# Expert passes of a hybrid decoder step: an up ring of eleven slabs instead of eight, and TensorE's up loop as two turns of 22 slabs

## The chip, the cores and the metric

The kernel runs on one core of one Trainium2 chip. The metric is the device time of one execution in microseconds. The kernel is timed in several runs, of which the median counts.

## The reference, cut to what matters

Two decoder layers work on 288 tokens (256 of a prompt, 32 sampled) of width 1024. Each has a recurrent mixer; the first ends in a dense SwiGLU, the second in a mixture of eight SwiGLU experts of width 2816, of which each token takes its best two. The change lies in the second:

```
def swiglu(h, w1, w3, w2):
    return (jax.nn.silu(h @ w1) * (h @ w3)) @ w2

def moe_swiglu(h, router, w1, w3, w2):
    logits = (h @ router).astype(jnp.float32)
    top_v, top_i = lax.top_k(logits, TOP_K)
    probs = jax.nn.softmax(top_v, axis=-1)
    gate = jnp.sum(jax.nn.one_hot(top_i, N_EXPERTS, dtype=jnp.float32) * probs[..., None], axis=-2)
    out = jnp.zeros(h.shape, jnp.float32)
    for e in range(N_EXPERTS):
        out = out + gate[..., e:e + 1] * swiglu(h, w1[e], w3[e], w2[e]).astype(jnp.float32)
    return out.astype(h.dtype)
```

All numbers are float32.

## The kernel before, in words

The code is written engine by engine: each `@block` function is the program of one engine, in the order in which it stands, and semaphores tie them together. `mix_out` ends a layer's mixer (the branch and output projections, the router's logits); `experts` follows it in the second layer.

**Passes.** `experts` makes one pass per expert. A pass gathers the tokens of its expert into `hg` (8 blocks of 128 channels x `cap` columns), runs the up loop, the down loop, and adds the result to `xT`. The caps of the eight passes are 91, 88, 73, 85, 76, 82, 79 and 70 columns (`CAPS`), and a matmul takes longer with more columns. Seven passes (`FIXED`) are written out one behind the other in TensorE's program, with `pe.Fori` loops inside; the eighth stands in a loop whose count is read at run time (passes for overflowing experts; one is run here).

**Weights.** An expert's weights lie in DRAM as 68 slabs: `UP_SLABS` = 44 of 128 x 1024 numbers (w1 and w3 by turns: slab 2f and 2f+1 give hidden block f), and `DOWN_SLABS` = 24, of which every third is 128 x 768. Up slabs go to `ring` (`RING` = 8 slots; slab n to slot n % 8), down slabs to `down_ring` in `proj` (`DRING` = 6 slots). Each slot has a semaphore that counts arrivals (`slab_in`, `down_in`); `slab_done` counts the slabs that TensorE has used, over both kinds. All loads are issued by SyncE, in one order, each behind a wait for the `slab_done` that frees its slot: the pass's down slabs 0 to 5, its up slabs 8 to 43, then the up slabs 0 to 7 of the following expert (4 to 7 first: `FREED`), then this pass's down slabs 6 to 23. A load that has to wait holds up all that stand behind it.

**TensorE's up loop.** `up` waits for a slab and for a free bank, then `narrow_products` does 16 matmuls of 64 output rows. As float32 each is two weight loads and two matmul rows in the trace, so a slab is 32 matmul rows. The loop is `Fori(0, 5)` over 8 slabs, and a tail of four slabs. Product n goes to `bank[n % 4]`. ScalarE takes the even ones (`silu`, signals `w1_free`), VectorE multiplies the odd ones into `hid` (`w3_free`). VectorE also prepares the next gather matrix during the first nine blocks (`choose`).

**Behind the up loop** come three transposes (`scatter_matrix`), the gather of the next pass's tokens (`gather_tokens`, into `HG` = banks 4 to 7) and the down loop, `Fori(0, 4)`: two output blocks a turn of three slabs each (176 matmul rows a turn), then `add_up` and `to_tokens` for the blocks of the turn before.

`y_ret` holds an input of the mixer's gate products (`xsum_up`) until the third pair of slabs in `mix_out` is done; `lora_w` holds sums for the first pair. In `experts` neither is used.

Of the kernel before, what the change touches and what calls it, by code (L numbers as in the profile page):

```python
# [22 lines left out]
D = 1024  # L23
# [66 lines left out]
UP_SLABS = 2 * FT  # L90
DOWN_SLABS = 24
# [129 lines left out]
def build(nc, xT_in, w_mix, w_lora, w_rank, w_gkup, vec_in, vecf_in, router_in, w_ff, s_ret, s_gla, s_rw,  # L221
# [132 lines left out]
    slab_in = [nc.alloc_semaphore(name=f"slab_in{s}") for s in range(RING)]  # L354
    slab_done = nc.alloc_semaphore(name="slab_done")
# [81 lines left out]

    def load_ff_slab(sp, e, j, s, done, n=KT):
# [11 lines left out]
    def narrow_products(pe, s, out, rhs, n=KT, k0=0, last=KT):  # L450

        for k in range(n):
            for c in range(2):
                mm = nc.tensor.matmul(out[64 * c:64 * c + 64], ring[:, s, k, 64 * c:64 * c + 64], rhs[:, k0 + k, :],  # L454
                                      start=(k0 + k == 0), stop=(k0 + k == last - 1))
        mm.then_inc(slab_done, 1)
# [1667 lines left out]
    def mix_out(nc, block, sig, layer, delta, joined):  # L2124
# [32 lines left out]
        def _(sp):  # L2157
            load_group(sp, S_RW_OUT, 1)
            load_first_group(sp, S_OUT)
# [300 lines left out]
    def experts(nc, block, sig, layer, merge, rs):  # L2460
# [48 lines left out]
        def _(sp):  # L2509
            def freed_up(p, n):  # L2510

                if n >= RING:
                    return count(p, FF_SLABS, FF0 + n - RING + 1)
                return count(p, FF_SLABS, FF0 - FF_SLABS + max(range(n, UP_SLABS, RING)) + 1)

            def load_up(p, e, n):
                load_ff_slab(sp, e, n, n % RING, freed_up(p, n))
# [10 lines left out]
            for q in range(FIXED):  # L2528
# [3 lines left out]
                for n in range(RING, UP_SLABS):  # L2532
# [4 lines left out]
                for n in FREED:  # L2537
# [5 lines left out]
            with sp.Fori(0, rest) as i:  # L2543
# [5 lines left out]
                for n in range(RING, UP_SLABS):  # L2549
                    load_up(p, e, n)  # L2550
                for n in FREED:
                    sp.wait_ge(slab_done, freed_up((i, FIXED + 1), n))
                    settle(sp)
                    sp.dma_start(ring[:, n], w_ff[following, n]).then_inc(slab_in[n], 16)
# [6 lines left out]
            for s in range(RING):  # L2561
                per = len(range(s, UP_SLABS, RING))
                fill = fills_before(layer, s) + fills(len(STREAM), s) + FIXED * per + 1
                sp.wait_ge(slab_in[s], rest * (per * 16) + fill * 16)
# [3 lines left out]
        def _(pe):  # L2568
# [741 lines left out]
```

## Time and profile before

| what | value |
|---|---|
| median of 3 runs | 2516.02 us (2513.42 to 2517.08) |
| profiled execution | 2513.11 us |
| its span in the profile | 2511.3 us |
| TensorE matmul busy | 2442.6 us, 97% |
| VectorE, ScalarE busy | 51%, 24% |
| granted TensorE clock | 0.997 of full |
| DMA moved in the span | 500.85 MB, mean 199 GB/s |

The profile is of one execution. The span runs from its first to its last instruction; the rest of the execution's time lies around it. TensorE's busy share counts a matmul as busy from its start to a modelled end, so gaps between matmuls are what shows of its waits. In the last quarter of the span the page shows DMA engines that are busy for eight to nine tenths or more, and 340 to 400 GB/s; before that they are busy for two to six tenths.

### The profile page before, as it was taken

To read this page: it belongs to the slowest core of one execution; us is meant where nothing else is said; L and a number is where in the kernel's file an instruction comes from. 1 tells how busy PE (TensorE), PEld (TensorE's weight loads), DVE (VectorE), ACT (ScalarE), POOL (GpSimd) and SP (SyncE) were. 2 spreads that over 40 slices of the span, in tenths; PEclk is the share of its full clock that TensorE was granted. 3 is DMA by queue.
4 is the path that set the end of the run, shared out by engine and by line. 5 is a ranking of instruction groups with operands and counts; after the bars stand their busy time and mean duration, and the time that the engine had idled before them with its cause. 6 is when DMAs were issued, how large, how long until landed. Compare 5 with 4: busy or idle time off the path is not lost. (4 is left out here: it accounts for less than half of the span.)

```text
span 2511.3 us, 103490 instructions
## 1 busy us (share of the span) xinstructions
PE 2442.6 (97%) x45930; PEld 2040.3 (81%) x45930; DVE 1291.6 (51%) x3328; ACT 609.9 (24%) x1798; POOL 0.2 (0%) x4
## 2 busy tenths in 40 slices
PE   9999999999999999999999999999999999999997
PEld 7987666666699999998766666678999899888986
DVE  7666666666686676756576666667311111111111
ACT  2233333433311101233333334421111111111111
POOL 0000000000000000000000000000000000000000
PEclk9999999999999999999999999999999999999999
DMA  6334442222243454333353222234899999999997
GB/s 248 111 136 161 151 133 88 83 83 79 99 154 136 153 173 144 128 124 139 129 168 129 84 78 77 83 112 154 341 342 390 393 392 370 402 372 374 402 388 274
DMA packets 146091, 500.85 MB, mean 199 GB/s; under 512 B 18784, under 2 KB 23520, under 8 KB 143360
## 3 DMA queue, kind: packets, MB, share of 16 engines
q1 hardware_dynamic: 145792, 496.44, 54.7%
q8 instruction: 239, 3.92, 0.6%
q14 instruction: 60, 0.49, 0.1%
HBM read 476.08 MB, written 20.29 MB: 198 GB/s over the span
## 5 line engine op out<-in xcount | busy, mean ns | idle before, releaser
L301 PE MATMUL psum<-hT,ring 128*64 128x144 f32 (+1 forms) x4568 | 457.4, 346 | 3.7 <-DVE hT L2421 1.7
L454 PE MATMUL psum<-work,ring 128*64 128x91 f32 (+7 forms) x11264 | 422.0, 234 | 15.7 <-issue 7.3
L454 PEld LDWEIGHTS psum<-work,ring 128*64 128x64 f32 x11264 | 404.7, 136 | 33.3 <-issue 23.8
L301 PEld LDWEIGHTS psum<-hT,ring 128*64 128x64 f32 x4568 | 293.3, 137 | 96.2 <-issue 12.1
L2958 DVE TENSOR_TENSOR work<-psum,work 128x91 f32<-128x91 f32 x176 | 44.6, 253 | 365.4 <-PE psum L454 365.2
L2661 PE MATMUL psum<-work,proj 128*64 128x91 f32 (+7 forms) x5632 | 208.9, 234 | 10.6 <-issue 9.2
L2661 PEld LDWEIGHTS psum<-work,proj 128*64 128x64 f32 x5632 | 202.3, 137 | 16.1 <-issue 10.3
L1767 ACT ACTIVATE work<-psum 128x256 f32<-128x256 f32 (+4 forms) x320 | 104.1, 362 | 349.7 <-PE psum L1678 84.8
L301 PE MATMUL psum<-work 128*64 128x144 f32 (+4 forms) x2096 | 154.1, 282 | 4.3 <-DVE work L1258 3.6
L301 PE MATMUL psum<-y_ret,work 128*64 128x144 f32 x2400 | 156.3, 286 | 0.5 <-DVE y_ret L531 0.5
L301 PEld LDWEIGHTS psum<-y_ret,work 128*64 128x64 f32 x2400 | 148.7, 137 | 0.9 <-issue 0.9
L2949 DVE TENSOR_TENSOR xT<-xT,psum 128x288 f32<-128x288 f32 x64 | 29.1, 455 | 228.6 <-PE psum L2672 227.6
L301 PEld LDWEIGHTS psum<-work 128*64 128x64 f32 (+2 forms) x2096 | 121.3, 136 | 30.6 <-issue 11.3
L2744 ACT ACTIVATE work<-psum 128x91 f32<-128x91 f32 x176 | 43.5, 247 | 377.5 <-PE psum L454 377.5
L301 PE MATMUL psum<-y_ret,ring 128*64 128x144 f32 (+1 forms) x1280 | 126.8, 332 | 2.5 <-ACT work L1767 2.5
L301 PEld LDWEIGHTS psum<-y_ret,ring 128*64 128x64 f32 x1280 | 79.5, 137 | 18.4 <-ACT work L1767 4.5
L323 PE MATMUL psum<-hT,ring 128*128 128x288 f32 x252 | 72.8, 408 | 0.0
L2748 ACT ACTIVATE work<-psum 128x91 f32<-128x91 f32 x64 | 15.9, 248 | 228.1 <-PE psum L2661 228.1
L1563 PEld LDWEIGHTS psum<-work 64*64 64x64 f32 x1408 | 47.3, 134 | 29.4 <-issue 17.7
L546 DVE TENSOR_TENSOR y_gla<-psum,y_gla 128x288 f32<-128x288 f32 x72 | 33.0, 458 | 72.8 <-PE psum L301 72.2
L301 PE MATMUL psum<-hT,work 128*64 128x144 f32 x928 | 68.8, 287 | 0.0
L518 DVE TENSOR_TENSOR work<-ring 128x512 f32<-128x512 f32 (+1 forms) x90 | 54.7, 608 | 19.0 <-PE psum L301 19.0
(513 smaller groups left out, 3733.5 us busy)
## 6 DMA issues: line engine op xcount, KB each, us to landing
ring<-w_ff_dram SPq DMA_DIRECT2D x424, 512.0 KB, 7.3
ring<-w_mix_dram SPq DMA_DIRECT2D x256, 512.0 KB, 4.1
proj<-w_ff_dram SPq DMA_DIRECT2D x128, 512.0 KB, 5.3
proj<-w_ff_dram SPq DMA_DIRECT2D x64, 384.0 KB, 5.6
work<-s_gla_dram SPq DMA_DIRECT2D x8, 1024.0 KB, 5.3
gla_s_out<-work SPq DMA_DIRECT2D x8, 1024.0 KB, 4.7
work<-s_ret_dram SPq DMA_DIRECT2D x8, 512.0 KB, 5.4
ret_s_out<-work SPq DMA_DIRECT2D x8, 512.0 KB, 3.0
```

Source lines behind the costliest of these rows:

```text
L301: last = nc.tensor.matmul(out[64 * c:64 * c + 64], weights[:, 64 * c:64 * c + 64], x, start=start, stop=stop)
L323: mm = (in_halves if self.narrow else nc.tensor.matmul)(out, ring[:, s, k, :], rhs[:, k, :], start=(k == 0), stop=(k == KT - 1))
L454: mm = nc.tensor.matmul(out[64 * c:64 * c + 64], ring[:, s, k, 64 * c:64 * c + 64], rhs[:, k0 + k, :], start=(k0 + k == 0), stop=(k0 + k = ...
L518: op.tensor_tensor(s1, a21, a22, ALU.add).then_inc(sig("wsum"), 1)
L546: nc.vector.tensor_tensor(c[:, 1:3, :], two(LAST_TWO[side]), c[:, 5:7, :], ALU.add).then_inc(sig("outer"), 1)
L1563: last = mm(unit(half(W, r), c), half(AT, 1 - r)[:, c], half(X, 1 - r)[:, c], start=True, stop=True)
L1767: return nc.scalar.activation(out, in_, func, **kw)
L2661: last = mm(DOWN[m][64 * h:64 * h + 64, 0:cap], down_ring[:, d, k, 64 * h:64 * h + 64], hid[:, KT * c + k, 0:cap], start=(KT * c + k == 0) ...
L2744: ac(act1[:, f % 2, :], bank[2 * f % 4][:, 0:CAP], ACT.Silu).then_inc(sig("w1_free"), 1)
L2748: ac(oT[:, m % 2, :], DOWN[m % 2][:, 0:CAP], cp).then_inc(sig("oT"), 1)
L2949: tt(xT[:, k, :], xT[:, k, :], ADD[m % 2][:, 0:T], ALU.add).then_inc(sig("added"), 1)
L2958: tt(hid[:, f, :], bank[(2 * f + 1) % 4][:, 0:CAP], act1[:, f % 2, :], ALU.mult).then_inc(sig("w3_free"), 1)
```

## The change

The up ring gets three more slots: `y_ret` (two) and `lora_w` (one). `UP_RING` = 11, slab n goes to slot n % 11, and 44 is four rounds of it. The three slots are filled for expert 1 in `mix_out`, behind a wait for the third gate pair (`join_done(BRANCH0 - 1)`). SyncE's order stays, with 11 for 8: down 0 to 5, up 11 to 43, the following expert's up 0 to 10, down 6 to 23. TensorE's up loop becomes `Fori(0, 2)` over 22 slabs (`TURN`) without a tail. The pairs of products still alternate between banks 0-1 and 2-3, but each eleventh pair goes to banks 6-7, which adds waits for "otok" and "added" of the pass before ahead of slab 20 of a turn. The gather is done in two halves (banks 4 and 5, then 6 and 7), with the wait for the last product's evacuation before the second half, where it had stood behind the gather. `narrow_products` uses `in_halves`, with the same matmuls in the same order (so their line is L303 in the changed kernel, not L454).

```diff
+UP_RING = 11
+TURN = 2 * UP_RING
...
+    extra_in = [nc.alloc_semaphore(name=f"extra_in{s}") for s in range(UP_RING - RING)]
+    up_in = slab_in + extra_in
...
+    extra_slots = [x.rearrange("p k n -> p (k n)")[:, D * j:D * j + D].rearrange("p (k n) -> p k n", k=KT)
+                   for x, j in ((y_ret[:, :, :], 0), (y_ret[:, :, :], 1), (lora_w[:, :, :], 0))]
+    up_slots = [ring[:, s] for s in range(RING)] + extra_slots
...
             load_group(sp, S_RW_OUT, 1)
+            if not dense:
+                sp.wait_ge(slab_done, join_done(BRANCH0 - 1))
+                for n in range(RING, UP_RING):
+                    sp.dma_start(up_slots[n], w_ff[1, n]).then_inc(up_in[n], 16)
             load_first_group(sp, S_OUT)
...
+        UP_BANK = [bank[6:8] if f % UP_RING == UP_RING - 1 else bank[0:2] if f % UP_RING % 2 == 0 else bank[2:4]
+                   for f in range(FT)]
...
-        FREED = 4, 5, 6, 7, 0, 1, 2, 3
...
-                if n >= RING:
-                    return count(p, FF_SLABS, FF0 + n - RING + 1)
-                return count(p, FF_SLABS, FF0 - FF_SLABS + max(range(n, UP_SLABS, RING)) + 1)
+                if n >= UP_RING:
+                    return count(p, FF_SLABS, FF0 + n - UP_RING + 1)
+                return count(p, FF_SLABS, FF0 - FF_SLABS + UP_SLABS - UP_RING + n + 1)
...
-                for n in range(RING, UP_SLABS):
+                for n in range(UP_RING, UP_SLABS):
                     load_up(p, e, n)
...
-                for n in FREED:
+                for n in range(UP_RING):
                     load_up((0, q + 1), following, n)
...
-            def gather_tokens(n, cap):
+            def gather_tokens(n, cap, evacuated=None):
 
                 pe.wait_ge(sig("picked"), n)
-                for j in range(2):
-                    for r in range(4):
-                        rows = slice(NS * r, NS * r + NS)
-                        mm(HG[r][:, CAP * j:CAP * j + cap], htok2[rows, j, :], gather[rows, 2, 0:cap], start=(j == 0),
-                           stop=False)
                 for r in range(4):
+                    if r == 2 and evacuated is not None:
+                        pe.wait_ge(sig("w3_free"), evacuated)
+                    if r % 2 == 0:
+                        for j in range(2):
+                            for q in range(r, r + 2):
+                                rows = slice(NS * q, NS * q + NS)
+                                mm(HG[q][:, CAP * j:CAP * j + cap], htok2[rows, j, :], gather[rows, 2, 0:cap],
+                                   start=(j == 0), stop=False)
...
-                narrow_products(pe, s, bank[n % 4][:, 0:cap], hg[:, :, 0:cap])
+                if n == TURN - 2:
+                    pe.wait_ge(sig("otok"), count(p, KT, 2))
+                    pe.wait_ge(sig("added"), count(p, KT, 2))
+                narrow_products(UP_BANK[f][n % 2][:, 0:cap], up_slots[s], hg[:, :, 0:cap])
...
-                with pe.Fori(0, UP_SLABS // RING) as g:
-                    for n in range(RING):
+                with pe.Fori(0, UP_SLABS // TURN) as g:
+                    for n in range(TURN):
                         up(p, cap, n, g)
-                for n in range(UP_SLABS // RING * RING, UP_SLABS):
-                    up(p, cap, n, 0)
                 scatter_matrix(p)
-                pe.wait_ge(sig("otok"), count(p, KT, 2))
-                pe.wait_ge(sig("added"), count(p, KT, 2))
-                gather_tokens(count(p, 1, 2), next_cap)
-                pe.wait_ge(sig("w3_free"), count(p, FT, FT + 2))
+                gather_tokens(count(p, 1, 2), next_cap, count(p, FT, FT + 2))
```

TensorE's program of pass 1, before: the loop body is 128 matmuls between the two branches, then the tail of 64, the transposes (L2648) and the gather.

```order
L2685 UNCONDITIONAL_BRANCH
...
L454 MATMUL psum<-work,ring 64x91 x32
L2638 REGISTER_ALU
L454 MATMUL psum<-work,ring 64x91 x32
...
L454 MATMUL psum<-work,ring 64x91 x32
...
L454 MATMUL psum<-work,ring 64x91 x32
L2685 REGISTER_ALU
L2685 COMPARE_AND_BRANCH
L454 MATMUL psum<-work,ring 64x91 x64
L2648 MATMUL psum<-table,work 91x128 x2
...
L2619 MATMUL psum<-work 128x88 x8
L2626 MATMUL psum<-work 64x88 x32
```

The same place in the changed program. Between the branches stand 352 matmuls now, with the slots in `y_ret` and `lora_w` among them, and nothing is left behind the loop but transposes and the gather in two halves.

```order
L2706 UNCONDITIONAL_BRANCH
...
L303 MATMUL psum<-work,ring 64x91 x32
...
L303 MATMUL psum<-work,y_ret 64x91 x32
L2656 REGISTER_ALU
L303 MATMUL psum<-work,lora_w 64x91 x16
...
L303 MATMUL psum<-work,lora_w 64x91 x16
L2706 REGISTER_ALU
L2706 COMPARE_AND_BRANCH
L2669 MATMUL psum<-table,work 91x128 x2
...
L2638 MATMUL psum<-work 128x88 x4
L2644 MATMUL psum<-work 64x88 x16
L2638 MATMUL psum<-work 128x88 x4
L2644 MATMUL psum<-work 64x88 x16
```

SyncE's queue between two passes, before: the last of the following expert's eight up slabs, and then this pass's down slabs from number 6 on.

```order
L441 DMA ring<-w_ff_dram 128x1024
L441 ISA
L441 DMA ring<-w_ff_dram 128x1024
L441 ISA
L441 DMA ring<-w_ff_dram 128x1024
L2525 ISA
L2525 DMA proj<-w_ff_dram 128x1024
L2525 ISA
L2525 DMA proj<-w_ff_dram 128x1024
...
L2525 DMA proj<-w_ff_dram 128x768
```

The same place now. The up slabs end with the three new slots, number 8 to 10 of the following expert, and they stand ahead of down slab 6.

```order
L2533 DMA ring<-w_ff_dram 128x1024
L2533 ISA
L2533 DMA ring<-w_ff_dram 128x1024
L2533 ISA
L2533 DMA y_ret<-w_ff_dram 128x1024
L2533 ISA
L2533 DMA y_ret<-w_ff_dram 128x1024
L2533 ISA
L2533 DMA lora_w<-w_ff_dram 128x1024
L2541 ISA
L2541 DMA proj<-w_ff_dram 128x1024
...
L2541 DMA proj<-w_ff_dram 128x768
```

What moved: down slab 6 stands behind eleven up slabs instead of eight.

## Rows read from the trace of the kernel before

**Rows 1.** The page, section 1: engine, busy us, share of the span, instructions
```profile
PE 2442.6 (97%) x45930; PEld 2040.3 (81%) x45930; DVE 1291.6 (51%) x3328; ACT 609.9 (24%) x1798; POOL 0.2 (0%) x4
```

**Rows 2.** The page's DMA issues: count, KB each, median us from issue to landing
```profile
ring<-w_ff_dram SPq DMA_DIRECT2D x424, 512.0 KB, 7.3
...
proj<-w_ff_dram SPq DMA_DIRECT2D x128, 512.0 KB, 5.3
proj<-w_ff_dram SPq DMA_DIRECT2D x64, 384.0 KB, 5.6
```

**Rows 3.** Groups by line, 1765 to 2511 us: busy, mean ns | idle before
```profile
L454 PE MATMUL psum<-work,ring 128*64 128x91 f32 (+7 forms) x11264 | 422.0, 234 | 15.7 <-issue 7.3 <-DMA ring<-w_ff_dram 5.2
```

**Rows 4.** Stretches: window, length, busy by engine, clock, DMA share, GB/s
```profile
1826.70:1865.10 38.40, 37.76 (x831) 34.44 (x829) 5.11 (x13) 4.07 (x17) 0.00 (x0) 1.00 0.92 319
...
1956.60:2009.80 53.20, 50.91 (x1410) 47.14 (x1409) 8.65 (x29) 8.03 (x26) 0.00 (x0) 1.00 1.02 406
2009.80:2043.80 34.00, 32.48 (x829) 28.87 (x827) 5.08 (x13) 4.03 (x16) 0.00 (x0) 1.00 1.00 383
```

**Rows 5.** Timeline of TensorE: start, us, line, count [idle before <- releaser]
```profile
1770.80 55.95 PE L454 MATMUL psum<-work,ring 128*64 128x91 f32 x1408 [0.20 <-issue]
...
1956.63 7.20 PE L454 MATMUL psum<-work,ring 128*64 128x73 f32 x219
1964.19 12.36 PE L454 MATMUL psum<-work,ring 128*64 128x73 f32 x357 [0.37 <-issue]
...
1987.03 10.00 PE L454 MATMUL psum<-work,ring 128*64 128x73 f32 x256 [0.24 <-DMA ring<-w_ff_dram]
1997.27 12.56 PE L454 MATMUL psum<-work,ring 128*64 128x73 f32 x320 [0.24 <-DMA ring<-w_ff_dram]
2009.76 0.65 PE L2648 MATMUL psum<-table,work 128*91 128x128 f32 x3
...
2022.22 5.80 PE L2661 MATMUL psum<-work,proj 128*64 128x73 f32 x176
...
2043.81 7.26 PE L454 MATMUL psum<-work,ring 128*64 128x85 f32 x190
...
2135.43 5.50 PE L454 MATMUL psum<-work,ring 128*64 128x76 f32 x160
...
2223.86 4.91 PE L454 MATMUL psum<-work,ring 128*64 128x82 f32 x130
2230.20 4.72 PE L454 MATMUL psum<-work,ring 128*64 128x82 f32 x126 [1.43 <-issue]
2236.62 41.50 PE L454 MATMUL psum<-work,ring 128*64 128x82 f32 x1120 [1.70 <-issue]
2279.61 1.36 PE L454 MATMUL psum<-work,ring 128*64 128x82 f32 x32 [1.48 <-DMA ring<-w_ff_dram]
...
2316.93 20.39 PE L454 MATMUL psum<-work,ring 128*64 128x79 f32 x576
...
2406.05 6.21 PE L454 MATMUL psum<-work,ring 128*64 128x70 f32 x194 [0.91 <-issue]
```

**Rows 6.** DMA queues (packets, MB, share): 1865-2405, 140-230, 2275.9-2277.0, 2277.0-2278.1 (two), 2278.1-2279.2
```profile
q8 instruction: 32, 0.52, 0.4%
...
q1 hardware_dynamic: 3501, 11.39, 35.0%
...
q1 hardware_dynamic: 126, 0.45, 102.8%
...
q1 hardware_dynamic: 118, 0.43, 98.4%
q8 instruction: 1, 0.02, 6.1%
...
q1 hardware_dynamic: 119, 0.44, 101.3%
```

**Rows 7.** Timeline of SyncE's queue, 1640 to 1760 us
```profile
1702.01 21.38 SPq L422 DMA_DIRECT2D ring<-w_mix_dram  x8
```

More of the change, by code:

```diff
@@ L448, in slab_products, with narrow_products @@
         mm.then_inc(slab_done, 1)
[L450 to L455, printed above, removed]
+    def narrow_products(out, slab, rhs):
+        for k in range(KT):
+            mm = in_halves(out, slab[:, k, :], rhs[:, k, :], k == 0, k == KT - 1)
         mm.then_inc(slab_done, 1)
@@ L2548, in _ @@
                     load_down(p, e, d)
-                for n in range(RING, UP_SLABS):
+                for n in range(UP_RING, UP_SLABS):
                     load_up(p, e, n)
-                for n in FREED:
+                for n in range(UP_RING):
                     sp.wait_ge(slab_done, freed_up((i, FIXED + 1), n))
                     settle(sp)
-                    sp.dma_start(ring[:, n], w_ff[following, n]).then_inc(slab_in[n], 16)
+                    sp.dma_start(up_slots[n], w_ff[following, n]).then_inc(up_in[n], 16)
                 for d in range(DRING, DOWN_SLABS):
@@ L2560, in _ @@
             sp.wait_ge(sig("stored"), 4 * 16)
[L2561 to L2564, printed above, removed]
+            for s in range(UP_RING):
+                per = UP_SLABS // UP_RING
+                sp.wait_ge(up_in[s], rest * (per * 16) + (up_fills(s) + FIXED * per + 1) * 16)
                 settle(sp)
@@ L2633, in up @@
                 i, done = p
-                s = n % RING
-                per = len(range(s, UP_SLABS, RING))
-                fill = fills_before(layer, s) + fills(len(STREAM), s) + done * per + n // RING + 1
-                pe.wait_ge(slab_in[s], turn * 16 + (i * (per * 16) + fill * 16))
-                pe.wait_ge(sig("w3_free" if n % 2 else "w1_free"), turn * (RING // 2) + count(p, FT, n // 2 + 1))
+                s, f = n % UP_RING, n // 2
+                per = UP_SLABS // UP_RING
+                fill = up_fills(s) + done * per + n // UP_RING + 1
+                pe.wait_ge(up_in[s], turn * (TURN // UP_RING * 16) + (i * (per * 16) + fill * 16))
+                pe.wait_ge(sig("w3_free" if n % 2 else "w1_free"), turn * UP_RING + count(p, FT, f + 1))
                 if n in (2, 3):
                     pe.wait_ge(sig("oT"), count(p, KT, n - 1))
-                narrow_products(pe, s, bank[n % 4][:, 0:cap], hg[:, :, 0:cap])
+                if n == TURN - 2:
+                    pe.wait_ge(sig("otok"), count(p, KT, 2))
+                    pe.wait_ge(sig("added"), count(p, KT, 2))
+                narrow_products(UP_BANK[f][n % 2][:, 0:cap], up_slots[s], hg[:, :, 0:cap])
             def scatter_matrix(p):
                 pe.wait_ge(sig("gated"), count(p, 1, 1))
-                pe.wait_ge(sig("w3_free"), count(p, FT, FT + 1))
+                pe.wait_ge(sig("w3_free"), count(p, FT, FT))
                 for i, (a, n) in enumerate(TILES):
```

9 lines of the change are left out of this document (6 added, 3 removed).

## The prediction

> **What bounds the kernel now.** I read the page first: TensorE is busy for 97% of the span [rows 1], so nothing but its own waits can be won. The change touches only the eight expert passes, which begin at 1770.80 us [rows 5] and fill nearly all that is left of the span, so nearly every view after that is of this stretch. The DMA issues on the page give the slab sizes: 512 KB, and 384 KB for every third down slab [rows 2]. The groups by line say that the up matmuls (L454) lost 15.7 us in idle time, of which 7.3 us is "issue" (nothing that the profile shows was waited for) and 5.2 us a wait for a ring slab [rows 3]. That is all that stands in front of these matmuls as gaps; smaller waits are smeared between them.
>
> The stretches tell which resource is full. In the up loop of pass 3 (73 columns) the DMA share is 1.02 at 406 GB/s, and in its down part 1.00 at 383 GB/s: the queue never rests there. In the down part of pass 1 it is 0.92, so it rests a little there [rows 4]. The timeline gives the price of a slab: in the starved middle of pass 3 eight slabs (256 matmul rows) start 10.24 us apart (1987.03 and 1997.27), so 1.28 us each [rows 5]. A pass loads 44 up and 24 down slabs. If the small ones cost as much as the large, that is 68 x 1.28 = 87.0 us. Pass 3 lasts from 1956.63 to 2043.81, 87.2 us [rows 5], so the **ledger of the queue closes** at this price, and 383 GB/s at a full share in the down part agrees (fewer bytes in the same time). Pass 5 lasts 88.4 us, pass 6 93.1 us, pass 7 89.1 us [rows 5].
>
> The second thing in the timeline is the "issue" gap. In pass 6 TensorE stops for 1.43 us after 130 matmul rows and for 1.70 us after 126 more [rows 5]. Each matmul row has a weight load beside it, so 128 rows are 256 instructions, and the instruction queue q8 moves 32 packets with 0.52 MB in six passes, 16 KB each [rows 6], which is 256 instructions of 64 bytes. So these gaps are waits for the next block of TensorE's program. In passes 2 to 7 that is 5.3 blocks a pass, while TensorE executes far more instructions than that: loop bodies are not fetched again. How long a block takes to come: pass 6 entered one at about 2223.9 and went on at 2230.20 (6.3 us), entered the next at 2230.20 and went on at 2236.62 (6.4 us); pass 3 entered one after 91 of its 219 rows, at 1959.6, and went on at 1964.19 (4.6 us); pass 1 runs through all 1408 rows without a gap, and 128 of its rows take 5.1 us, so there it was at most 5.1 us [rows 5]. I take 5.3 us, with 4.6 and 6.4 as ends.
>
> **The ring, part by part.** Eleven slots instead of eight let three more up slabs (3.84 us of queue time) wait ready. They do not make the queue faster, and its order matters: the next pass's eleven up slabs are issued before down slab 6 of this pass. In a pass that the queue bounds, every pass still has to load 68 slabs between the same two points, so it stays at 87.0 us. Worked through for pass 3: its last up slab begins when it lands, 1997.27 plus 288 of 320 rows, 2008.6. Down slab 6 lands 8 + 1 slabs later, 2020.1, and TensorE takes it at 2022.22 [rows 5]. With eleven slots the last up slab lands three slabs earlier, 2004.7, but down slab 6 twelve slabs after that, again at 2020.1; TensorE, 3.8 us earlier, now wants it at 2018.4 and **waits 1.7 us in the down loop**. The rest is given back behind it. So what the ring can return is the time by which a pass exceeds 87.0 us because of the queue: pass 3 0.2, pass 5 1.4, pass 7 2.1; pass 6 the 1.48 us that it waited for its last up slab, and 0.9 us smeared over 1120 rows (36.9 ns each against 36.1 ns in the 126 rows before) [rows 5]. Passes 4 and 8, whose gaps are not taken apart here, I take like pass 5. Together 8.9 us; the lower end is 0. I take half, 4.4 us, since the down wait above eats into each.
>
> **The three extra loads ahead of pass 1** stand behind a wait that is one slab earlier than what the S_OUT loads wait for. Those eight loads are released one by one over 21.4 us [rows 7], 2.7 us or more each against 1.28 us of queue time, and each is used eight slabs after the release: 3.84 us are hidden there, 0. Pass 8 loads three slabs more that nobody uses, behind the up slabs and ahead of down slab 6: 3.84 us of queue, which cancels against the three loaded early.
>
> **The turn of 22 slabs.** The old body is 8 slabs, 256 matmul rows, two block borders, and the five turns reuse it. The new body is 704 rows, 5.5 blocks, walked once with fetching and once, if it stays, without: **3.5 more borders and 2.5 more blocks a pass** (a block in the tail of four slabs goes away). At a border TensorE waits 5.3 us less the time that 128 rows take. Where TensorE is the bound: pass 1 (5.1 us) 0.2, passes 2 and 4 (88 and 85 columns, between pass 1 and pass 6's 4.8 us, so 4.9) 0.4 each, together 1.0 x 3.5 = 3.5 us. In the passes that the queue bounds the wait itself is covered: at 73 columns four slabs take 4.2 us and the queue needs 5.1 us for them; if that cover went, it would be 1.1 x 3.5 = 3.9 us a pass. But there the block's packet takes queue time. In the 1.1 us around the one at 2277 us the slab queue's share falls from 102.8 to 98.4, while the block's own packet takes 6.1%, 1.07 us of one engine [rows 6]. Against the mean of the stretches before and after (102.8 and 101.3) it is 3.65%, which over 1.1 us is 0.64 us of one engine. If every slab waits for that engine a block costs 0.64 us; pass 3, with five blocks and a ledger that closes to 0.2 us, says 0.04 us. I take 0.3 us, between the two: 2.5 x 5 passes x 0.3 = 3.8 us (0.5 to 8.0).
>
> TensorE's program has four turns of looping less a pass; nothing shows at the old loop ends (1408 rows in one piece in pass 1 [rows 5]), so 0. The gather in two halves has the same matmuls; its new wait is for the vector product of the last slab, which runs beside the transposes (0.65 us [rows 5]) and the first half of the gather: 0. The third bank pair (6 and 7) for each eleventh product waits for "otok" and "added" of the pass before, done some 20 slabs earlier: 0.
>
> **Sum.** -4.4 + 3.5 + 3.8 = +2.9 us. The profiled execution took 2513.11 us (span 2511.3 us), so 2516.0 us by its own time; it lies 2.9 us under the median of the runs, 2516.02 us, and by the median it is **2519 us**.
>
> **Does the body stay?** In the stretch from 140 to 230 us TensorE repeats a loop of 261 matmuls with their loads (4.3 blocks by the same count), and no instruction packet moves at all: the only queue there is q1 [rows 6]. So at least 4.3 blocks stay; 5.6 are needed. By the Trainium skill (Runtime: NRT & Kernel Launch, Instruction fetch mechanics) TensorE's instruction memory holds 128 KiB, 2048 instructions, in 16 KiB blocks, while the same section says that the memory is only two such lines and that a taken branch out of the window stalls for a fetch. By the first the new body stays and the sum is as above; by the second each turn would be fetched again. The 4.3 blocks speak against the second.
>
> **Rivals.** *The body is fetched again in the second turn.* Then 44 slabs are eleven blocks at 5.3 us and the jump back waits for a whole one: 58.3 + 5.3 = 63.6 us for an up loop that takes 53 to 57 us now, about 8 us more in each of eight passes: 2580 us. For it: nothing as long as 5.6 blocks has been looped. Chance 0.06.
>
> *Faster.* The ring returns all 8.9 us and the borders are hidden (a block takes 5.0 us or less, as in pass 1): 2507 us. For it: in pass 6 both gaps come early, while the ring is full and the queue rests, and the wait for the last slab comes late; three more slots join them. Against it: the down wait worked out above. Chance 0.25.
>
> *Slower, by the blocks.* With up to eleven slabs on the way instead of eight, and in the middle of the up loop rather than at its start, a block comes later. At 5.8 us the borders of passes 1, 2, 4 and 6 cost (0.7 + 0.9 + 0.9 + 1.0) x 3.5 = 12.3 us, the packets 5 us, less 4.4 us: +12.9, 2529 us. It decides from about 5.5 us on. Pass 6 showed 6.3 and 6.4 us. With 6.4 us and 0.64 us a packet it is +24 us. Chance 0.31.
>
> **Chances.** The forecast (within a few microseconds of no change) has 0.38. 0.2% is 5 us, about what a measurement of this kernel can tell from no change. Faster 0.25, same 0.38, slower 0.31 + 0.06 = 0.37. The range reaches from the full return of the ring, 2507, to a little past the slower case, 2532; outside lie the refetching case, 0.06, and the tails of the two others, about 0.1. The likeliest case's own range is 2511 to 2521.
>
> **What would show it.** The gaps before L454 (now at L303) from a ring slab should nearly vanish from the up loops of passes 3, 5 and 7, and new waits for a proj slab appear before the third block of the down loop. q8 should move about 7.9 packets a pass instead of 5.3, all the added ones in the first 22 slabs, none in the second 22. In pass 1 small "issue" gaps should appear every 128 rows of the first turn, and pass 3 should still last 87 us. The prediction is wrong if queue-bound passes fall well below 87 us (then the ledger is no floor), if packets show up in the second turn, or if the gaps at borders are well above 1 us in passes 1 and 2.

## The result, and the profile after

The changed kernel takes 2528.55 us (median of 9 runs, 2521.68 to 2534.41), the kernel before 2514.55 us (9 runs, 2511.73 to 2517.08). The ratio is 1.0054, with an interval of 1.0042 to 1.0066: the change **costs 13.6 us**. The forecast was 2519 us with a range of 2507 to 2532: the time lies in the range, but 9.5 us above the forecast, where the rival "slower, by the blocks" (2529) stood. A few executions of some kernels in this document ran at a lower clock or far longer than the rest; they are left out of every time and ratio. The profiled execution has a span of 2526.7 us and a granted clock of 0.993.

The page after the change, TensorE, the instruction queue and the down matmuls:

```profile
PE 2438.6 (97%) x45930; PEld 2046.1 (81%) x45930; DVE 1290.6 (51%) x3328; ACT 609.1 (24%) x1798; POOL 0.2 (0%) x4
...
q8 instruction: 260, 4.26, 0.7%
...
L2682 PE MATMUL psum<-work,proj 128*64 128x91 f32 (+7 forms) x5632 | 212.8, 237 | 12.8 <-issue 6.8
```

TensorE is busy for 4 us less than in [rows 1] in a span that is 15.4 us longer, so its idle time grew by 19.4 us. The view of waits for 1765 to 2530 us (engine, line, releaser: us in total, times, longest) names it:

```profile
PE psum L303 <- issue: 34.1, 29, 3.0
...
PE psum L2682 <- issue: 6.8, 6, 2.0
...
PE psum L2682 <- DMA proj<-w_ff_dram: 5.4, 6, 2.4
```

In [rows 3] the up matmuls waited 7.3 us for "issue" and 5.2 us for a ring slab. Now it is 34.1 us for "issue", and no wait for a slab is left in any up loop. The ring does what it was made for, but the waits for "issue", which the prediction put down to blocks of TensorE's program, grew by far more than the ring removed. And the waits for down slabs are 5.4 us, where the same view of the kernel before has 1.0 us.

TensorE's timeline in passes 1 and 3 (start, us, line, count [idle before <- releaser]):

```profile
1782.79 1.88 PE L303 MATMUL psum<-work,y_ret 128*64 128x91 f32 x42 [0.22 <-issue]
...
1788.64 8.38 PE L303 MATMUL psum<-work,ring 128*64 128x91 f32 x205 [0.64 <-issue]
...
1800.21 0.93 PE L303 MATMUL psum<-work,y_ret 128*64 128x91 f32 x18 [1.43 <-issue]
...
1962.71 6.69 PE L303 MATMUL psum<-work,ring 128*64 128x73 f32 x204
1969.67 1.87 PE L303 MATMUL psum<-work,ring 128*64 128x73 f32 x52 [0.27 <-issue]
...
1976.39 0.92 PE L303 MATMUL psum<-work,lora_w 128*64 128x73 f32 x22 [2.50 <-issue]
...
1982.77 4.21 PE L303 MATMUL psum<-work,ring 128*64 128x73 f32 x125 [0.53 <-issue]
1988.28 1.11 PE L303 MATMUL psum<-work,ring 128*64 128x73 f32 x28 [1.30 <-issue]
...
2003.44 8.30 PE L303 MATMUL psum<-work,ring 128*64 128x73 f32 x256
...
2028.67 7.30 PE L2682 MATMUL psum<-work,proj 128*64 128x73 f32 x176 [0.54 <-DMA proj<-w_ff_dram]
```

Each of the "issue" gaps stands some 128 rows (or twice that) behind the one before it, and all in the first turn. From one gap to the next is taken here as the time that a block took to come: in pass 1 5.85 us (1782.79 to 1788.64) and then 11.57 us for two; in pass 3 6.7, 6.4 and 5.5 us. Other passes spread further: in pass 5 the gaps end at 2149.77, 2154.89 and 2162.24 us, so 5.1 and 7.4 us. The second turn of pass 3 runs without a gap (256 rows from 2003.44 in 8.30 us, 32.4 ns each). The DMA queues of pass 3, its first turn (1962.7 to 1992.3) and its second (1992.3 to 2014.7), say the same:

```profile
q1 hardware_dynamic: 3022, 10.88, 96.0%
q8 instruction: 5, 0.08, 1.1%
...
q1 hardware_dynamic: 2457, 8.95, 101.5%
```

Five blocks in the first turn, none in the second. The first turn also shows the slab queue at 96.0% only. Stretches of the changed kernel (window, length, busy by engine, clock, DMA share, GB/s): the up loop of pass 1, up loop and down part of pass 3, two stretches inside its first turn, and one down turn each of passes 3, 5 and 8:

```profile
1771.40:1830.30 58.90, 56.61 (x1408) 56.06 (x1408) 12.38 (x55) 6.22 (x23) 0.00 (x0) 1.00 0.95 360
1962.70:2014.70 52.00, 47.40 (x1409) 46.78 (x1408) 8.62 (x29) 7.69 (x26) 0.00 (x0) 0.97 0.99 383
2014.70:2052.20 37.50, 34.67 (x831) 30.91 (x827) 5.08 (x13) 4.34 (x16) 0.00 (x0) 0.95 1.00 385
1960.00:1975.00 15.00, 13.62 (x377) 12.59 (x374) 3.83 (x10) 3.20 (x9) 0.00 (x0) 1.00 0.96 363
1975.00:1990.00 15.00, 11.79 (x305) 11.48 (x306) 2.47 (x8) 1.23 (x5) 0.00 (x0) 0.89 0.98 370
...
2028.70:2036.00 7.30, 7.30 (x178) 7.25 (x180) 0.00 (x0) 0.25 (x1) 0.00 (x0) 0.79 0.97 378
...
2212.20:2219.90 7.70, 7.69 (x178) 7.64 (x180) 0.00 (x0) 0.25 (x1) 0.00 (x0) 0.78 0.99 374
...
2487.30:2495.50 8.20, 8.16 (x178) 8.09 (x180) 0.00 (x0) 0.25 (x1) 0.00 (x0) 0.68 0.92 328
```

The two 15 us windows of the kernel before, for comparison, and then when a block comes: the first 5 us of pass 1 before, and a stretch between two gaps of pass 1 after:

```profile
1960.00:1975.00 15.00, 14.52 (x442) 14.10 (x438) 4.54 (x13) 1.73 (x7) 0.00 (x0) 1.00 1.02 398
1975.00:1990.00 15.00, 14.07 (x380) 12.74 (x376) 1.87 (x7) 1.49 (x6) 0.00 (x0) 1.00 1.03 410
...
1770.80:1776.00 5.20, 5.20 (x131) 5.20 (x133) 4.23 (x29) 0.49 (x2) 0.00 (x0) 1.00 0.49 147
...
1783.00:1788.60 5.60, 5.01 (x126) 4.82 (x122) 0.97 (x4) 0.49 (x2) 0.00 (x0) 1.00 1.03 414
```

Where the queue moved 398 and 410 GB/s it now moves 363 and 370. At the start of an up loop the ring is full and the queue has little to do (a share of 0.49 in pass 1 before); the blocks of the long turn come later, at a share of 1.03.

**The gather** has the same matmuls as before, but in two halves they take longer. Behind the up loop of pass 1, before and after:

```profile
1827.07 0.74 PE L2619 MATMUL psum<-work 32*128 32x88 f32 x16
1827.75 2.65 PE L2626 MATMUL psum<-work 128*64 128x88 f32 x64
...
1830.72 0.74 PE L2638 MATMUL psum<-work 32*128 32x88 f32 x8
1831.40 1.44 PE L2644 MATMUL psum<-work 128*64 128x88 f32 x32
1832.76 0.68 PE L2638 MATMUL psum<-work 32*128 32x88 f32 x8
1833.37 1.43 PE L2644 MATMUL psum<-work 128*64 128x88 f32 x32
```

Eight of the 32-partition rows take as long as sixteen did (0.68 us to the next line). Before, four groups of 32 partitions came by turns, now two. From the first transpose to the first down matmul it is 4.31 us in place of 3.54 in pass 1, and 0.75 to 0.77 us more in each of passes 1 to 3 and 5 to 7: up to 6 us in the eight passes, wherever TensorE is what bounds.

**The clock.** The three windows of the kernel after at 0.79, 0.78 and 0.68 show that after a wait TensorE comes back at a lower granted clock: 176 rows take 7.30 us that took 5.80 us in [rows 5]. An estimate of the whole from the mean clocks: 0.7% of a span of 2526.7 us is 17.7 us of full clock that was not granted, 0.3% of 2511.3 us is 7.5 us, so at most some 10 us of the 15.4 us lie in the clock (the rounding of the clocks leaves 2 to 3 us either way). It is hardly a cause of its own beside the waits: in these windows it falls behind them.

The passes by the timeline, from start to start, in us (pass 8: to the end of its last down matmul; ring of ten: the second experiment):

| pass | 1 | 2 | 3 | 4 | 5 | 6 | 7 | 8 | sum |
|---|---|---|---|---|---|---|---|---|---|
| before | 94.3 | 91.6 | 87.2 | 91.6 | 88.4 | 93.1 | 89.1 | 89.3 | 724.6 |
| after | 97.2 | 94.1 | 89.5 | 91.5 | 92.6 | 91.2 | 92.5 | 90.4 | 739.0 |
| ring of ten | 94.3 | 92.1 | 86.4 | 90.7 | 88.8 | 89.4 | 88.8 | 86.6 | 717.1 |

Six of the eight passes lose, those bound by TensorE (1, 2) and those bound by the queue (3, 5, 7) among them. Of the 2.9 us in pass 1 the up loop lost 3.1 us (59.0 in place of 55.9) and the gather 0.8, and the down loop, which has no gap now, gave back 0.9.

### The profile page after: what moved, and what is told of

Its sections match the earlier page's. It is cut to its first block and busy times, and to the rows that moved or that the text cites. A ratio compares the mean times of both kernels' runs of the same rounds, so it can differ in the third digit from the quotient of the medians.

```text
span 2526.7 us, 103445 instructions
## 1 busy us (share of the span) xinstructions
PE 2438.6 (97%) x45930; PEld 2046.1 (81%) x45930; DVE 1290.6 (51%) x3328; ACT 609.1 (24%) x1798; POOL 0.2 (0%) x4
## 5 line engine op out<-in xcount | busy, mean ns | idle before, releaser
L303 PE MATMUL psum<-hT,ring 128*64 128x144 f32 (+1 forms) x4568 | 457.5, 346 | 3.7 <-DVE hT L2435 1.7
L303 PE MATMUL psum<-work,ring 128*64 128x88 f32 (+8 forms) x8800 | 350.7, 238 | 21.6 <-issue 21.5
L303 PEld LDWEIGHTS psum<-hT,ring 128*64 128x64 f32 x4568 | 293.4, 137 | 96.1 <-issue 12.0
L303 PEld LDWEIGHTS psum<-work,ring 128*64 128x64 f32 x8800 | 335.4, 138 | 25.8 <-issue 24.7
L303 PE MATMUL psum<-work 128*64 128x144 f32 (+4 forms) x2096 | 154.2, 282 | 4.3 <-DVE work L1268 3.6
L303 PE MATMUL psum<-y_ret,work 128*64 128x144 f32 x2400 | 156.3, 286 | 0.5 <-DVE y_ret L541 0.5
L303 PEld LDWEIGHTS psum<-y_ret,work 128*64 128x64 f32 x2400 | 148.8, 137 | 0.9 <-issue 0.9
L303 PEld LDWEIGHTS psum<-work 128*64 128x64 f32 (+2 forms) x2096 | 121.4, 136 | 30.6 <-issue 11.3
L303 PE MATMUL psum<-y_ret,ring 128*64 128x144 f32 (+1 forms) x1280 | 126.9, 332 | 2.5 <-ACT work L1777 2.5
L303 PEld LDWEIGHTS psum<-y_ret,ring 128*64 128x64 f32 x1280 | 79.6, 137 | 18.4 <-ACT work L1777 4.5
L303 PE MATMUL psum<-work,y_ret 128*64 128x91 f32 (+7 forms) x2048 | 80.1, 233 | 5.1 <-issue 5.1
L303 PEld LDWEIGHTS psum<-work,y_ret 128*64 128x64 f32 x2048 | 76.0, 136 | 6.3 <-issue 6.1
L1573 PEld LDWEIGHTS psum<-work 64*64 64x64 f32 x1408 | 47.3, 134 | 29.4 <-issue 17.7
```

The source lines that it names most:

```text
L303: last = nc.tensor.matmul(out[64 * c:64 * c + 64], weights[:, 64 * c:64 * c + 64], x, start=start, stop=stop)
L1573: last = mm(unit(half(W, r), c), half(AT, 1 - r)[:, c], half(X, 1 - r)[:, c], start=True, stop=True)
```

## The experiments

**Two theories.** *The blocks* (the prediction's slower rival): what costs is the longer stretch of program that each pass walks through for the first time; the ring itself gains. *The order*: what costs is that eleven up slabs instead of eight stand ahead of down slab 6, which showed as the 5.4 us of waits for `proj`. A pass's program for the up loop counts here as slabs written out: 12 before (8 + 4), 22 after; each adds 64 instructions, so ten slabs are 2.5 blocks a pass and 20 in eight passes.

**1. Blocks without the ring.** In the kernel before, the first turn of eight slabs is written out ahead of the loop: 20 slabs, two blocks a pass more.

```diff
-                with pe.Fori(0, UP_SLABS // RING) as g:
-                    for n in range(RING):
+                for n in range(RING):
+                    up(p, cap, n, 0)
+                with pe.Fori(0, UP_SLABS // RING - 1) as g:
+                    for n in range(RING, 2 * RING):
```

> The kernel before (ring of eight, same loads) with the first turn of eight slabs written out ahead of a loop of four turns: two more blocks of TensorE's program a pass, nothing else. Theory A (the program blocks cost the time: waits at block borders, and their packets in the queue): two of the 2.6 added blocks, so 8 to 12 us above the kernel before, TensorE's issue waits in front of the up matmuls about 20 us instead of 7.3 us. Theory B (the ring's three slabs ahead of down slab 6 cost it, the program is harmless): no change, 0 to 2 us.

Measured: 2520.77 against 2512.96 us, ratio 1.0030 (1.0020 to 1.0041). The waits of its expert passes:

```profile
PE psum L454 <- issue: 22.9, 18, 2.4
...
PE psum L454 <- DMA ring<-w_ff_dram: 2.1, 11, 0.2
```

So blocks alone cost 7.5 us (5.0 to 10.3), 0.47 us each. The "issue" waits grew by 15.6 us, but the profiled execution, 2526.81 us, is one of the longest of its kernel, 13.7 us above the profiled one of the kernel before; and with eight slots TensorE had been waiting for slabs anyway: 3.1 of those 5.2 us are gone here.

**2. The ring without the blocks.** Ten slots need no long turn: 44 slabs are four turns of ten and a tail of four, 14 slabs written out, half a block a pass more than before. The early loads, the gather in halves and the third bank pair are in it too. Since 44 is not a multiple of ten, the following expert's slabs are again loaded in the order in which their slots come free (`FREED`).

```diff
-UP_RING = 11
+UP_RING = 10
...
-        UP_BANK = [bank[6:8] if f % UP_RING == UP_RING - 1 else bank[0:2] if f % UP_RING % 2 == 0 else bank[2:4]
+        UP_BANK = [bank[6:8] if f % 5 == 4 else bank[0:2] if f % 5 % 2 == 0 else bank[2:4]
...
-                with pe.Fori(0, UP_SLABS // TURN) as g:
-                    for n in range(TURN):
+                with pe.Fori(0, UP_SLABS // UP_RING) as g:
+                    for n in range(UP_RING):
                         up(p, cap, n, g)
+                for n in range(UP_SLABS // UP_RING * UP_RING, UP_SLABS):
+                    up(p, cap, n, 0)
```

> A ring of ten (two slots more than before), with the up loop as four turns of ten slabs and a tail of four: half a block more than before instead of 2.6. Theory A: within 4 us of the kernel before, issue waits about 10 us. Theory B: two of the three slabs stand ahead of down slab 6, so 8 to 10 us above before, with the waits for a proj slab at 3 to 5 us.

Measured: 2506.62 us, ratio 0.9976 (0.9968 to 0.9985), **6.0 us faster than before** and the best kernel of this study. Its waits, and then its stretches of pass 3 (up loop, down part):

```profile
PE psum L302 <- issue: 10.1, 11, 2.3
...
PE psum L2682 <- DMA proj<-w_ff_dram: 2.9, 6, 1.1
PE psum L302 <- DMA ring<-w_ff_dram: 1.5, 7, 0.3
```

```profile
1959.88:2010.96 51.08, 49.41 (x1409) 46.58 (x1408) 8.62 (x29) 7.98 (x26) 0.00 (x0) 1.00 1.02 402
2010.96:2046.32 35.36, 33.39 (x832) 29.52 (x828) 5.10 (x13) 4.08 (x17) 0.00 (x0) 1.00 1.02 395
```

The up loop is 2.1 us shorter than in [rows 4] and the down part 1.4 us longer; pass 3 as a whole goes from 87.2 to 86.4 us. That is the ledger of the queue at work, as it was worked out for eleven slots (0.8 us of the 1.4 us is the gather in halves). The gain comes from passes that were longer than the ledger: pass 6 93.1 to 89.4, pass 8 89.3 to 86.6. Not all of it need be the ring's: in pass 6 the "issue" gaps of the up loop fell from 3.1 to 0.6 us, since block borders fell elsewhere; over all passes such waits hardly changed (17.9 to 18.7 us).

**3. The order.** In the changed kernel, up slabs 8 to 10 of the following expert go behind down slab 11.

```diff
-                for n in range(UP_RING):
+                for n in range(RING):
                     load_up((0, q + 1), following, n)
-                for d in range(DRING, DOWN_SLABS):
+                for d in range(DRING, 2 * DRING):
+                    load_down(p, e, d)
+                for n in range(RING, UP_RING):
+                    load_up((0, q + 1), following, n)
+                for d in range(2 * DRING, DOWN_SLABS):
```

> The changed kernel with SyncE's order changed: the following expert's up slabs 0 to 7, then down slabs 6 to 11, then up slabs 8 to 10, then down 12 to 23. Theory A: the waits for a proj slab fall from 5.4 us to about 1 us, but the issue waits of the up loop stay near 27 us, and the time stays within 5 us of the changed kernel (10 us or more above before). Theory B: most of the 13.6 us comes back, 2 to 5 us above before.

Measured: 2539.64 us, ratio 1.0112 (1.0097 to 1.0127), worse by another 14.6 us. Its waits:

```profile
PE psum L303 <- issue: 34.8, 31, 2.7
PE psum L2692 <- DMA proj<-w_ff_dram: 19.0, 10, 2.7
```

The waits for down slabs grow from 5.4 to 19.0 us, where the first theory had expected about 1 us and the second most of the loss back. Down slabs 6 to 11 wait for slots that TensorE frees only as it works through the down loop, and SyncE's queue holds up the three up slabs, whose slots are free, behind them. Slabs that can go at once belong ahead of slabs that must wait. The order theory falls with this order and with experiment 2, which has ten slabs ahead of down slab 6 and gains.

**4. Fewer instructions for the same work.** In the changed kernel the up matmuls are 128 wide, which halves their instructions.

```diff
-            mm = in_halves(out, slab[:, k, :], rhs[:, k, :], k == 0, k == KT - 1)
+            mm = nc.tensor.matmul(out, slab[:, k, :], rhs[:, k, :], start=(k == 0), stop=(k == KT - 1))
```

> The changed kernel with up matmuls of 128 output rows instead of two of 64: half as many instructions a slab, so the first turn has 2.75 blocks instead of 5.5. A matmul row then takes about twice as long (16 rows of the final sums took 4.16 us for 288 columns, so 82 ns at 91 columns, 1.32 us a slab against 1.27 us). Theory A: the border waits nearly vanish, since a block lasts 10 us; passes bound by the queue fall towards 87 us and the others gain the borders and lose 2 us: 2508 to 2518 us. Theory B: slower than the changed kernel by the longer matmuls, 2530 to 2535 us.

Measured: ratio 1.0744 (1.0726 to 1.0763), about 2700 us (2697.55 to 2703.04 in three runs). The profiled execution took 2772.80 us: its granted clock is 1.00 up to 2400 us and falls to 0.54 in the last 140 us of the passes. The "issue" waits in front of the up matmuls fall to 1.2 us, as they should by the blocks. But the work itself became dearer, as the group by line and the start of pass 1 show:

```profile
L465 PE MATMUL psum<-work,ring 128*128 128x91 f32 (+7 forms) x4096 | 513.3, 293 | 1.2 <-issue 1.2
...
1771.36 14.52 PE L465 MATMUL psum<-work,ring 128*128 128x91 f32 x128 [0.23 <-issue]
```

At the full clock 128 rows of 91 columns take 14.36 us (to the next line, 1785.72), 112 ns a row, in place of two narrow rows at 39.7 ns (1408 in 55.9 us); the 125 ns a row of the group hold the stretch at the lower clock. By the ratio, the wide rows cost 171 us more than the narrow ones of the changed kernel, and 33 us more still for the waits they saved: 204 us over 5632 rows, 36 ns a row more than two narrow ones. My price for a wide row, 82 ns, was wrong, and this way to fewer blocks is closed.

**5 and 6. Half the up bytes.** Both kernels load only the first four of the eight channel blocks of each up slab in the passes and leave out the rest; TensorE does the same matmuls. The edit in the changed kernel (the kernel before passes 4 to its `load_ff_slab`):

```diff
-                sp.dma_start(up_slots[n % UP_RING], w_ff[e, n]).then_inc(up_in[n % UP_RING], 16)
+                sp.dma_start(up_slots[n % UP_RING][:, 0:4], w_ff[e, n, :, 0:4]).then_inc(up_in[n % UP_RING], 16)
```

> The kernel before, but each up slab of the passes (other than the first eight) loads only its first 4 of 8 blocks, so that the queue is never full in the up loop; TensorE multiplies what the slot still holds in the other half. Theory A (a program block comes late because the weight loads fill the DMA engines): no waits for slabs and no issue waits in front of the up matmuls at two borders a pass; about 40 us below the kernel before, 2470 to 2480 us. If a block takes its time whatever the queue does: the 7 us of issue waits stay.

> The changed kernel with the same halved up loads. Theory A: the borders cost nothing when the queue is not full, so it takes the same time as the kernel before with halved loads (within 3 us) and its issue waits in the up loop fall from 27 us more than before to about none. If a block takes 5 us whatever the queue does: about 20 us of issue waits stay and it is 10 to 20 us slower than the kernel before with halved loads.

Measured: before 2466.73 us (0.9820, 0.9803 to 0.9837), after 2479.61 us (0.9865, 0.9851 to 0.9879). By the ratios the difference between them is 11.3 us, where the theory had expected less than 3. But not all of it is blocks: with TensorE the bound (no pass of the two waits for an up slab) the gather in halves costs its 0.75 us in each (28.4 in place of 23.1 us over the first seven passes), 6.0 us in eight. That leaves some 5 us, about 0.25 us for each of the 20 blocks, with no ring waits for the ring to return. Pass 3 of the second, up loop and down part:

```profile
1958.40:2005.80 47.40, 45.74 (x1409) 45.14 (x1408) 8.61 (x29) 7.69 (x26) 0.00 (x0) 1.00 0.79 259
2005.80:2040.40 34.60, 33.27 (x831) 29.30 (x827) 5.07 (x13) 4.35 (x16) 0.00 (x0) 1.00 0.85 311
```

At a share of 0.79 the up matmuls of all passes wait 8.5 us for "issue" instead of 34.1 (3.0 us in the kernel before with half the bytes). The up loop of pass 1 takes 55.9 us, as in the kernel before, instead of 59.0: there a block costs nothing without the full queue. In pass 3 it still costs (44.9 us without, 47.4 us with the long turn): 128 rows of 73 columns take 4.1 us, and its blocks took 5.4 and then 4.3 us. So a block's cost has two parts, and the full queue adds the larger: 0.25 us a block without it, 1.1 us with it and the deeper ring (experiment 7).

**7. The blocks on top of the good ring.** The kernel of experiment 2, with its first turn of ten written out: 24 slabs, 20 blocks more.

```diff
-                with pe.Fori(0, UP_SLABS // UP_RING) as g:
-                    for n in range(UP_RING):
+                for n in range(UP_RING):
+                    up(p, cap, n, 0)
+                with pe.Fori(0, UP_SLABS // UP_RING - 1) as g:
+                    for n in range(UP_RING, 2 * UP_RING):
...
-                if n == UP_RING - 2:
+                if n % UP_RING == UP_RING - 2 and n < 2 * UP_RING:
```

> The ring of ten with its first turn of ten slabs written out ahead of a loop of three: 2.5 more program blocks a pass than the ring of ten, about as many as the changed kernel has. Theory A: those blocks cost 8 to 11 us, so the 6 us that the ring of ten gained become a loss of 2 to 5 us against the kernel before. Theory C (the ring of eleven is worse for its eleventh slab or for its third bank pair, not for its blocks): no change against the ring of ten, 5 to 7 us below before.

Measured: 2528.41 us, ratio 1.0065 (1.0049 to 1.0081). Its waits:

```profile
PE psum L302 <- issue: 30.0, 27, 2.3
...
PE psum L2682 <- DMA proj<-w_ff_dram: 2.2, 3, 1.0
```

It loses 22 us to the ring of ten (more than either theory expected), 1.1 us a block, and lands where the changed kernel did, with fewer waits for down slabs than that. The eleven slots, the slot in `lora_w` and the turn of 22 as such are not needed to explain the loss.

**8. A ring of twelve.** Three turns of twelve and a tail of eight: 20 slabs, 12 blocks more than the ring of ten, and two slots more (the second new one in `lora_w`). An even number of pairs a turn needs no third bank pair.

```diff
-UP_RING = 10
+UP_RING = 12
...
-        UP_BANK = [bank[6:8] if f % 5 == 4 else bank[0:2] if f % 5 % 2 == 0 else bank[2:4]
+        UP_BANK = [bank[0:2] if f % 2 == 0 else bank[2:4]
```

> A ring of twelve (four slots more, a second one in the same dead buffer as the eleventh), three turns of twelve slabs and a tail of eight: two more program blocks a pass than before, like the kernel with the peeled turn, and more ring than the changed kernel. Theory A: the blocks cost about 7 us and the ring gives back 4 to 6 us, so 0 to 5 us above before. Theory B (slabs ahead of down slab 6 cost it): worse than the changed kernel, 15 us or more above before.

Measured: 2518.50 us, ratio 1.0026 (1.0017 to 1.0035): 12.6 us above the ring of ten, 1.05 us a block. Waits of L302 for "issue" are 21.5 us.

**9. All 44 slabs written out** in the kernel before: eight blocks a pass more, 64 in all.

```diff
-                with pe.Fori(0, UP_SLABS // RING) as g:
-                    for n in range(RING):
-                        up(p, cap, n, g)
-                for n in range(UP_SLABS // RING * RING, UP_SLABS):
+                for n in range(UP_SLABS):
```

> The kernel before (ring of eight) with all 44 up slabs written out and no loop: eight more program blocks a pass, 64 in all. If a block costs the same wherever it is crossed, at 0.5 us (as the peeled turn says) 30 us above before, at 1.1 us (as the peeled ring of ten says) 70 us. If only the first turn's borders matter (ring full, queue at rest) and later borders are covered by the wait for slabs, it saturates at 10 to 20 us above before.

Measured: 2574.42 us, ratio 1.0240 (1.0225 to 1.0255), 60 us, 0.94 us a block. Waits and the instruction queue of the expert passes:

```profile
PE psum L454 <- issue: 74.5, 63, 2.8
...
q8 instruction: 108, 1.77, 0.8%
```

108 packets against 60 in experiment 1 over the same passes: 48 more, as six blocks a pass should give. The blocks' price does not shrink with their number; it is twice that of experiment 1.

**10. A gentler order for the ring of ten.** Its last two up slabs go behind down slabs 6 and 7.

```diff
-                for n in FREED:
+                for n in FREED[:RING]:
                     load_up((0, q + 1), following, n)
-                for d in range(DRING, DOWN_SLABS):
+                for d in range(DRING, DRING + 2):
+                    load_down(p, e, d)
+                for n in FREED[RING:]:
+                    load_up((0, q + 1), following, n)
+                for d in range(DRING + 2, DOWN_SLABS):
```

> The ring of ten with SyncE's order changed a little: the following expert's eight first-freed up slabs, then down slabs 6 and 7, then the two last up slabs, then down 8 on. Down slab 6 no longer stands behind more up slabs than in the kernel before, and the two up slabs wait only until two down slabs are used. If the waits for proj slabs (2.9 us) are what the ring gives back: 1 to 3 us below the ring of ten. If holding up slabs behind down slab 7 lets the queue rest, as in the coarser change of order: 0 to 5 us above it.

Measured: 2517.22 us, ratio 1.0014 (1.0005 to 1.0024), 9.5 us slower than without, where 1 to 3 us less or up to 5 us more had been expected. Its waits (in a profiled execution of 2512.63 us, one of its shortest):

```profile
PE psum L2692 <- DMA proj<-w_ff_dram: 11.3, 14, 2.1
PE psum L302 <- issue: 9.2, 12, 1.4
```

The waits for down slabs rise from 2.9 to 11.3 us here too.

Together, by slabs written out in a pass (intervals above; every ring of ten or more has the gather in halves, those of eight have not, so each price compares like with like):

| kernel | slots | slabs written out | ratio to before | a block costs |
|---|---|---|---|---|
| ring of ten | 10 | 14 | 0.9976 | |
| before | 8 | 12 | 1 | |
| ring of twelve | 12 | 20 | 1.0026 | 1.05 us (to ring of ten) |
| first turn written out | 8 | 20 | 1.0030 | 0.47 us (to before) |
| the change | 11 | 22 | 1.0054 | 1.2 us (to ring of ten) |
| ring of ten, first turn written out | 10 | 24 | 1.0065 | 1.1 us (to ring of ten) |
| all written out | 8 | 44 | 1.0240 | 0.94 us (to before) |

## Why the prediction was right in its range and wrong in its sum

**What the number is worth.** 2528.55 us lies in the range of 2507 to 2532 because the range reached out to the slower rival; the sum itself, 2519, and the likeliest case's own range, 2511 to 2521, missed it. That the rival's 2529 fits is in part luck: it put 3.2 and 3.5 us on the borders of passes 4 and 6, which came out 0.1 and 1.8 us shorter than before, and only packets (5 us in five passes) on the queue-bound ones, of which passes 3, 5 and 7 lost 2.3, 4.1 and 3.4 us.

**What held.** The mechanism of most parts: the waits for ring slabs vanished; q8 moved five packets in pass 3's first turn and none in its second, 47 in six passes, 7.8 each against 7.9 foretold; the body of 5.6 blocks stays. The new wait for a down slab stands where it was put, before the third block of pass 3's down loop (0.54 us after the change, behind an "issue" gap of 1.75 us in the turn before; 1.10 us in the ring of ten; 1.7 us worked out). The early loads and the third bank pair show no wait of their own; no run has them alone. The queue's ledger is a floor: no pass of any kernel with whole slabs is more than 1 us below 87.0 us (86.4 the lowest).

**The step that failed** is the one on the borders: "in the passes that the queue bounds the wait itself is covered". It priced the 20 added blocks at 3.5 + 3.8 = 7.3 us. They cost some 22 to 24 us. This comes from two sides: the ring of ten with 20 blocks more loses 22 us; and the change's 13.6 us plus what the ring returns, net of the gather (below), is 22 to 24 us. Three things were wrong in it:

- The cover. Passes 3, 5 and 7 took 89.5, 92.6 and 92.5 us, not the 87 to 89 of a queue that never rests. While TensorE stands at a border with every slot full, no slot comes free and no load can be issued: the slab queue fell to 96.0% in the first turn of pass 3. What TensorE lost there the queue lost too, and at 1.28 us a slab it does not catch up. That this is the way in which the cover goes is argued from the order of the loads and these shares; no run takes it apart. A queue-bound pass covers a wait only as long as slots are free, and the deeper ring starts each pass with all eleven full. With eight slots, where TensorE waits for slabs anyway, the cover is half real in experiment 1: 0.47 us a block against 1.1 us; with all slabs written out it is 0.94 us, so most of it is gone there too.
- The block's time. 5.3 us was taken, 5.5 to 6.7 us was seen in passes 1 and 3 (5.8 in pass 1), 5.1 to 7.4 us in pass 5. Pass 1 was priced at 0.2 us a border, 0.7 us in all, and its up loop lost 3.1 us; that of pass 2 lost 1.9 us (57.1 in place of 55.3) against 1.4 us. This is the rival's condition, "from about 5.5 us on", and its cause, a full queue in the middle of the up loop, is shown by pass 1 with half the bytes (55.9 us).
- The clock. After a wait of 2.42 us, up to 2212.21, the granted clock was 0.78 for the next 7.7 us. The mean of the run fell from 0.997 to 0.993. No term of the sum had this.

**The gather's term** was put at 0, since "the gather in two halves has the same matmuls". The same matmuls took 0.75 us a pass more, up to 6 us in all, in every kernel with the halves.

**The ring's term** was too small. The ring of ten returns 6.0 us net, with four blocks more than before at 0.5 to 1.1 us each, so by this estimate 8 to 10 us, and that is after the gather in halves has taken its part. My upper bound was 8.9 us and I took half of it, "since the down wait eats into each". The bound itself or more, with the down wait and all, is what came back. For eleven slots alone it is not measured: no turn was tried that gives them without more blocks.

By the Trainium skill (Runtime: NRT & Kernel Launch, Instruction fetch mechanics) crossing a 16 KiB boundary is mostly hidden, because the sequencer fetches the next block while the current one runs. Here that is so in pass 1 of the kernel before, whose blocks come while the queue is not full, and of both kernels with half the bytes (no gap in the up loop); beside a full queue it is not: the 29 gaps of the changed kernel cost 34.1 us. The same section's two-line memory is contradicted by the second turn without a packet.

**What stays open** is how the 22 to 24 us divide between the wait at the border, the queue's rest and the lower clock: the three come together in each run, and half the bytes removes two of them at once (both of its profiled executions have a mean clock of 0.997). Why a block comes later beside a full queue, and why rows of two partition groups take as long as rows of four, no run takes apart. Also open is why a down slab of 384 KB costs the queue about as much as one of 512 KB; the ledger uses that without explaining it.

## What to carry to other kernels

Count what a change does to the program's length: where a loop body grows, each further 256 instructions of TensorE's program are fetched once a visit, and here each fetch cost 0.5 to 1.2 us beside a saturated DMA queue and about 0.25 us beside one that was not full, together more than the three slots were worth. So pick the depth of a ring by the loop that it allows (ten slots in turns of ten won 6 us, eleven in turns of 22 lost 14 us).

"Covered by a full queue" holds only while the queue has somewhere to put its data: ask of each wait of the consumer whether the buffers are full at that moment. In one queue of loads, those whose slots are free go ahead of those that have to wait.

"The same matmuls" in another order are not the same time: where a change regroups small matmuls, compare that stretch in the trace, however short it is.

## What was not expected of the hardware

After waits of 2.3 to 3.5 us, one gap or two close together, TensorE's granted clock fell to a mean of 0.68 to 0.79 over the next 7 to 8 us (full is 2.4 GHz, so part of that stretch ran at 1.2 GHz), and 176 matmul rows took 7.30, 7.66 and 8.11 us where the same rows take 5.80, 6.03 and 5.60 us in the kernel before. So the wait of 2.4 us in the down loop of pass 5 costs about 4 us: the 176 rows behind it took 7.66 us, 1.6 us more than the next 176.

A float32 matmul row with 128 output rows and 91 columns took 112 ns at the full clock, where a row of 64 output rows takes 39.7 ns: two narrow matmuls beat one wide one by some 1.4 times.

Sixteen float32 matmul rows over 32 partitions that went round four groups of 32 partitions took 0.68 us; eight that went round two groups took 0.68 us as well.
